# Three small VectorE steps of an attention stage put one to three steps later or earlier, and the last weight unit of the program computed in two column parts

## The chip, the cores and the metric

The kernel runs on one NeuronCore of one Trainium2 chip. The metric is the device time of one execution, in microseconds, as the median of several runs. Lower is better. Engines are named as the profile names them: PE (TensorE, matmuls) with PEld for its weight loads, DVE (VectorE), ACT (ScalarE), POOL (GpSimd), SP (SyncE, which issues the weight transfers).

## The reference, cut to what matters

A two-layer transformer on 256 tokens of width 1024, all in f32. Each layer is a SwiGLU FFN, a mixer and a second SwiGLU FFN, each followed by a layer norm of `ALPHA * x + f`. The mixer of layer 0 is the NSA attention, that of layer 1 a differential attention. The change touches the NSA attention and the very last layer norm.

```python
def post_norm(x, f, g, b):
    return layer_norm(DEEPNORM_ALPHA * x + f, g, b)      # after every FFN and mixer

# nsa_mixer, per block of queries: three branches
s = einsum('bqghd,bcgd->bqghc', qc, k_cmp)               # compressed: 15 keys per group
p_cmp = softmax(where(vis, s, NEG)) * any(vis)
o_cmp = einsum('bqghc,bcgd->bqghd', p_cmp, v_cmp)
o_slc = softmax(masked qr . k_sel) @ v_sel               # here every block is selected
o_win = softmax(masked qr . k_win) @ v_win
o = g[0] * o_cmp + g[1] * o_slc + g[2] * o_win
```

The FFN is `0.5 * (silu(x @ w_gate) * (x @ w_up)) @ w_down` with an inner width of 2816.

## The kernel before

**Tiling.** The 256 tokens are two tiles of 128 (`tok` 0 and 1). Every large matrix product is made from three fp32r matmuls: activations and weights are split in a high and a low part (`xt_hi`, `xt_lo`, `ht_hi`, `ht_lo`; `w_hi`, `w_lo`), and `three()` (L1429) issues hi·hi, hi·lo and lo·hi, 512 columns wide, into a PSUM bank of `acc`. Weights come in units of 1 MB (L438), four slots deep; ACT makes `w_hi` (L663), DVE makes `w_lo` (L961). Nine stages run one after the other: ffn0, nsa_in, nsa_out, ffn1, kv, ffn2, diff_q, diff_out, ffn3. Between nsa_in and nsa_out lies the NSA attention. Each engine has its own program, written out by hand; the engines meet at semaphores only, and each runs its instructions in order.

**The NSA attention.** `NSA_JOBS` holds 24 jobs: eight for tile 0 (two heads each), sixteen for tile 1 (one head each). `job_steps` (L114) runs 27 steps. In step i, PE computes the scores of job i (L1779, L1784, L1788), transposes the probabilities of job i-2 (`turn_p`, L1481) and multiplies those of job i-3 by the values (L1650). DVE takes the negated row maximum of job i (`maxima`, L1125), ACT takes four exponentials with their sums (`exps`, L774; they write `probs`, which lies in the tile `norm_gb`) and copies the transposed probabilities of job i-2 out of PSUM (`copy_p`, L680). Scores of job i wait for the exponentials of job i-3.

**The compressed branch of tile 1** rides along in those steps. PE computes its scores in eight pairs of heads, shared out over steps by the table `SECOND_COMPRESSED` (L1726, into bank `aux` 1). DVE adds a mask and subtracts the maximum in step 4 (`compressed_shift(1)`, L1229, L1232, L1233), ACT takes the exponential in step 4 (`compressed_exp(1)`, L867), PE transposes it in step 7, DVE copies it to `pct` (L1240). For each tile `compressed_share` (L1246 to L1248) makes the factor by which the compressed output is scaled: that of tile 0 in step 4, that of tile 1 in step 6. `split_beside(3)` cuts the rotated queries of tile 1 in high and low parts: ACT the high one in step 3 after its exponentials (L694), DVE the low one in step 3 as well (L992).

**Where a set of heads ends** (jobs 3, 7, 15, 23), DVE runs `nsa_mix` (L1257 to L1274): it inverts the sums, scales the three branches out of PSUM banks `aux` 1, `acc` 2 and `acc` 3 into SBUF, tells PE that these banks are read (`turn_read`), and adds them up. PE starts the next set with `nsa_first` (L1755), which waits for `turn_read`. The first of these mixes stands in step 6.

**POOL** meanwhile splits the four weight units of nsa_out (L567 for the high part, L568 for the low part), 16 times each.

**The end.** In ffn3, PE runs the last four units of w_down for tile 1 by halves: columns 0 to 511 of all four into `acc` 2, then columns 512 to 1023 into `acc` 3. `last_norm` (L1085) adds the residual for each half (L1094), takes `bn_stats` of it (L1097), joins the two with `bn_aggr` (L1099), and subtracts the mean while POOL makes the inverse root of the variance (L544, L547). The last line (L1108) and the output transfers (L509) follow.

Of the kernel before, what the change touches and what calls it, by code (L numbers as in the profile page):

```python
# [21 lines left out]
ALU = mybir.AluOpType  # L22
# [4 lines left out]
P = 128  # L27
# [29 lines left out]
G_FULL = FF // 512  # L57
# [41 lines left out]

SECOND_COMPRESSED = {1: range(0, 3), 2: range(3, 6), 3: range(6, 8)}  # L100

# [129 lines left out]
def build_program(nc, x_in, x_turned, const, squares_in, w_gate_up, w_downs, ln_g, ln_b, w_in, w_out_a,  # L231
                  cmp_pos, cmp_w1, cmp_b1, cmp_w2, w_kv, w_q, lambdas, subln_g, w_out_b, out):
    with ExitStack() as ctx:
# [29 lines left out]
        half_pow = sb("half_pow", [P, 4])  # L263
        stats = sb("stats", [P, 2, 6])
        mean_var = sb("mean_var", [P, TOKS, 2])
# [390 lines left out]
        def _(act):  # L656
# [213 lines left out]
            for i, sc, tr, pv in job_steps(NSA_JOBS):  # L870
# [4 lines left out]
                if sc:  # L875
                    exps("nsa", NSA_JOBS, i, 0)
                if i == 4:
                    compressed_exp(1)
# [70 lines left out]
        def _(dve):  # L949
# [135 lines left out]
            def last_norm():  # L1085
# [3 lines left out]
                for half, cols in enumerate(halves):  # L1089
                    if half == 0:  # L1090
                        dve.wait_ge(half_full, 1)
                    else:
                        filled(dve, "ffn3", G_FULL + 1, tok)
                    ins = dve.scalar_tensor_tensor(y[:, tok, cols], x[:, tok, cols], ALPHA, acc[:, 2 * tok + half],  # L1094
                                                   ALU.mult, ALU.add)
                    link(ins)
                    ins = dve.bn_stats(stats[:, half, :], y[:, tok, cols])  # L1097
                link(ins)
# [178 lines left out]
            for i, sc, tr, pv in job_steps(NSA_JOBS):  # L1277
                if sc:
                    maxima(NSA_JOBS, i, 0, score_bank[i % 3])
                if i == 0:  # L1280
                    copy_queries(1)
                if i == 4:
                    compressed_shift(1)
                if i in PCT_STEPS:
                    copy_compressed(PCT_STEPS.index(i))
                if i == 3:
                    split_beside(3)
                if i in (4, 6):
                    compressed_share(i // 2 - 2)
                if pv >= 0 and NSA_JOBS[pv][3]:  # L1290
# [137 lines left out]
        def _(pe):  # L1428
# [116 lines left out]
            def ffn_stage(stage, turn_rest, operand, next_x):  # L1545
# [35 lines left out]
                for i, js in enumerate(DOWN_GROUPS):  # L1581
# [10 lines left out]
                    if stage == "ffn3" and i == len(DOWN_GROUPS) - 1:  # L1592

                        for half in range(2):
                            for j in js:
                                ins = emit(n0 + UNITS_GU + j, j, 1, [half])
                                if half:
                                    ins.then_inc(unit_used, 1)
                            if not half:
                                ins.then_inc(half_full, 1)  # L1600
# [3 lines left out]
                    if i == len(DOWN_GROUPS) - 1:  # L1604
                        finish(1, ins)

            def nsa_out_stage():
# [427 lines left out]
```

## Time and profile before

| what | us |
|---|---|
| median of 3 runs (1036.62 to 1036.65) | 1036.63 |
| the profiled execution | 1036.8 |
| its span, from the first to the last instruction | 1034.6 |
| PE busy in it | 1016.9 |
| DVE busy / ACT busy / POOL busy | 580.0 / 480.5 / 108.0 |
| mean granted TensorE clock | 0.996 |

Times below are microseconds from the start of the span unless marked ns. A matmul's record is longer than the room it takes on PE, because matmuls are pipelined: the distance from one start to the next is what counts. The granted clock is given in parts of full speed. "idle before" and the engine and line behind "<-" say how long an engine had been idle before a row and who ended that.

### The profile page before, as it was taken

Reading aid. Unit: us, or ns where it says so; the run is one execution under the profiler, and the core shown is the slowest. Engines: PE = TensorE matmul, PEld = TensorE weight load, DVE = VectorE, ACT = ScalarE, POOL = GpSimd, SP = SyncE. Lnnn points to the kernel's source line nnn. Section 1 sums busy time; section 2 is a strip of 40 time slices with the busy share of each in tenths; the row PEclk is TensorE's granted clock in tenths of the full one; section 3 lists DMA queues with packets and bytes.
Section 4 is the critical chain, followed back from the end, with each engine's and each line's share of the span. In section 5 each row is a group of like instructions: output and inputs, shape, how many; then the busy total and the mean of one; then the engine's idle time right before and its main releaser. Section 6 shows DMA issues by size and latency. Waiting matters only on the chain.

```text
span 1034.6 us, 12671 instructions
## 1 busy us (share of the span) xinstructions
PE 1016.9 (98%) x4964; PEld 839.6 (81%) x4964; DVE 580.0 (56%) x583; ACT 480.5 (46%) x650; POOL 108.0 (10%) x141
## 2 busy tenths in 40 slices
PE   9999999999999999999999999999998999999997
PEld 7888888888788888888888888888887778888885
DVE  6655443764855654463575554462588774555443
ACT  7443432445673544452443434452467655554330
POOL 0010000223910100000012000000025110000000
PEclk9999999999999999999999999999999999999999
DMA  9676554650312655455446655455442354455431
GB/s 340 235 259 241 199 180 153 204 203 1 124 41 84 240 207 199 165 174 192 162 163 235 222 197 200 163 191 174 163 163 82 123 203 163 164 202 208 160 118 41
DMA packets 75835, 179.47 MB, mean 173 GB/s; under 512 B 3264, under 2 KB 5456, under 8 KB 75792
## 3 DMA queue, kind: packets, MB, share of 16 engines
q1 hardware_dynamic: 73312, 170.21, 47.2%
q0 software_dynamic: 2480, 8.66, 2.5%
q8 instruction: 30, 0.49, 0.2%
q14 instruction: 13, 0.11, 0.0%
HBM read 177.81 MB, written 1.05 MB: 173 GB/s over the span
## 4 chain that ended last, share of the span: by engine, by line
PE 94%; DVE 2%; ACT 2%; issue 1%; POOL 0%; POOLq 0%; DVEq 0%; ACTq 0%
PE acc L1431 27%; PE acc L1433 27%; PE acc L1432 27%; PE trb L1481 5%; PE acc L1650 2%; ACT norm_gb L774 1%; PE acc L1534 1%; PE acc L1537 1%; PE acc L1538 1%; PE aux L1694 1%; PE aux L1755 0%; PE acc L1784 0%; PE aux L1660 0%; DVE neg_max L1125 0%; ACT y L794 0%
## 5 line engine op out<-in xcount | busy, mean ns | idle before, releaser
L961 DVE TENSOR_TENSOR w_lo<-raw,w_hi 128x2048 fp32r<-128x2048 f32 x148 | 337.7, 2284 | 212.8 <-ACT w_hi L663 212.5
L663 ACT ACTIVATE w_hi<-raw 128x2048 fp32r<-128x2048 f32 x148 | 282.2, 1908 | 201.7 <-PE acc L1433 199.3
L1431 PE MATMUL acc<-w_hi,xt_hi 128*128 128x512 f32 x896 | 355.8, 397 | 1.8 <-DVE xt_lo L976 1.2
L1433 PE MATMUL acc<-w_hi,xt_lo 128*128 128x512 f32 x896 | 348.3, 389 | 0.0
L1432 PE MATMUL acc<-w_lo,xt_hi 128*128 128x512 f32 x896 | 347.5, 388 | 0.0
L1433 PEld LDWEIGHTS acc<-w_hi,xt_lo 128*128 128x128 f32 x896 | 168.2, 188 | 35.4
L1431 PEld LDWEIGHTS acc<-w_hi,xt_hi 128*128 128x128 f32 x896 | 168.4, 188 | 34.7 <-issue 2.5
L1432 PEld LDWEIGHTS acc<-w_lo,xt_hi 128*128 128x128 f32 x896 | 168.6, 188 | 31.6
L1431 PE MATMUL acc<-w_hi,ht_hi 128*128 128x512 f32 x352 | 139.6, 397 | 0.0
L1433 PE MATMUL acc<-w_hi,ht_lo 128*128 128x512 f32 x352 | 139.0, 395 | 0.0
L1432 PE MATMUL acc<-w_lo,ht_hi 128*128 128x512 f32 x352 | 139.0, 395 | 0.0
L546 POOL TENSOR_SCALAR rstd<-total 128x1 f32<-128x1 f32 x11 | 11.3, 1026 | 742.1 <-ACT aux L704 742.1
L1433 PEld LDWEIGHTS acc<-w_hi,ht_lo 128*128 128x128 f32 x352 | 66.0, 187 | 16.1
L1432 PEld LDWEIGHTS acc<-w_lo,ht_hi 128*128 128x128 f32 x352 | 66.0, 188 | 15.9
L1431 PEld LDWEIGHTS acc<-w_hi,ht_hi 128*128 128x128 f32 x352 | 66.0, 187 | 15.8
L716 ACT ACTIVATE ht_hi<-trb 128x512 f32 (+2 forms) x48 | 26.7, 557 | 107.8 <-PE trb L1481 107.8
L1037 DVE TENSOR_TENSOR ht_lo<-trb,ht_hi 128x512 f32 (+2 forms) x48 | 30.5, 642 | 71.9 <-ACT ht_hi L716 71.9
L712 ACT ACTIVATE y<-acc 128x512 f32<-128x512 f32 (+1 forms) x48 | 26.9, 563 | 69.7 <-PE acc L1433 69.7
L1032 DVE SCALAR_TENSOR_TENSOR y<-y,acc 128x512 f32<-128x512 f32 (+1 forms) x48 | 30.7, 639 | 39.4 <-ACT y L712 39.4
L704 ACT ACTIVATE aux<-y,total 128x1024 f32<-128x1024 f32 x11 | 12.3, 1120 | 54.8 <-DVE total L1013 54.8
L675 ACT ACTIVATE xt_hi<-trb 128x512 fp32r<-128x512 f32 x24 | 13.2, 596 | 41.9 <-PE trb L1481 41.9
L1481 PEld LDWEIGHTS trb<-id_r,y 128*128 128x128 f32 x200 | 24.9, 139 | 7.5 <-DVE y L992 0.6
(208 smaller groups left out, 806.5 us busy)
## 6 DMA issues: line engine op xcount, KB each, us to landing
raw<-ffn_gate_up SPq DMA_DIRECT2D x84, 1024.0 KB, 5.3
raw<-ffn_w_down SPq DMA_DIRECT2D x44, 1024.0 KB, 4.9
raw<-w_kv SPq DMA_DIRECT2D x8, 1024.0 KB, 5.0
raw<-w_in SPq DMA_DIRECT2D x6, 1024.0 KB, 5.9
raw<-ffn_gate_up SPq DMA_DIRECT2D x16, 256.0 KB, 6.1
raw<-w_out_a SPq DMA_DIRECT2D x4, 1024.0 KB, 4.8
raw<-w_q SPq DMA_DIRECT2D x4, 1024.0 KB, 5.1
raw<-w_out_b SPq DMA_DIRECT2D x4, 1024.0 KB, 5.7
```

Of the source, the lines that this page charges most:

```text
L663: act.activation(w_hi[:, slot, 0:k * c], raw[:, slot, 0:k * c], ACT.Copy).then_inc(hi_ready, 1)
L675: act.activation(dst, turned, ACT.Copy).then_inc(tr_hi, 1)
L712: act.activation(sil[:, tok, 0:c], acc[:, 2 * tok, 0:c], ACT.Silu).then_inc(silu_done, 1)
L716: act.activation(ht_hi[:, bass.ds(4 * g, k), tok * P:(tok + 1) * P], trb[:, bank, 0:k * P].rearrange("p (k c) -> p k c", c=P), ACT.Copy).t ...
L961: dve.tensor_tensor(w_lo[:, slot, 0:k * c], raw[:, slot, 0:k * c], w_hi[:, slot, 0:k * c].bitcast(F32), ALU.subtract).then_inc(lo_ready, 1)
L1032: dve.scalar_tensor_tensor(h_nat[:, tok, 0:c], sil[:, tok, 0:c], 0.5, up, ALU.mult, ALU.mult).then_inc(acc_free, 1)
L1037: dve.tensor_tensor(ht_lo[:, bass.ds(4 * g, k), tok * P:(tok + 1) * P], trb[:, bank, 0:k * P].rearrange("p (k c) -> p k c", c=P), ht_hi[:, ...
L1431: pe.matmul(out_ap, s_hi, hi, start=first, stop=False)
L1432: pe.matmul(out_ap, s_hi, lo, start=False, stop=False)
L1433: return pe.matmul(out_ap, s_lo, hi, start=False, stop=last)
L1481: ins = pe.transpose(trb[:, bank, j * P:(j + 1) * P], b, ident)
L1650: ins = pe.matmul(acc[:, 2 + m, (h % per_turn) * width:(h % per_turn + 1) * width], turned_probs[:, j % 2, k * P:(k + 1) * P], v_of(h, m, ...
```

## The change

Within the NSA steps, for DVE: `compressed_shift(1)` moves from step 4 to step 5, `split_beside(3)` from step 3 to step 4 (now behind the maximum of job 4), `compressed_share(0)` from step 4 to step 2, `compressed_share(1)` from step 6 to step 7. For ACT, `compressed_exp(1)` moves from step 4 to step 5. For PE, the second tile's compressed scores are shared over steps 2, 3 and 4 in place of 1, 2 and 3.

At the end, the last of the four units computes columns 512 to 767 first, into `acc` 3, signals, and then columns 768 to 1023 into bank `aux` 0, from zero. DVE adds the residual to all 512 columns after the first of them (columns 768 to 1023 then still lack that unit's share), takes the statistics of columns 512 to 767, then adds the `aux` part to the last 256 columns and takes their statistics. `bn_aggr` joins three groups.

```diff
-SECOND_COMPRESSED = {1: range(0, 3), 2: range(3, 6), 3: range(6, 8)}
+SECOND_COMPRESSED = {2: range(0, 3), 3: range(3, 6), 4: range(6, 8)}
...
-        stats = sb("stats", [P, 2, 6])
+        stats = sb("stats", [P, 3, 6])
... (ACT, in the NSA steps)
-                if i == 4:
+                if i == 5:
                     compressed_exp(1)
... (DVE, last_norm)
                 for half, cols in enumerate(halves):
-                    if half == 0:
-                        dve.wait_ge(half_full, 1)
-                    else:
-                        filled(dve, "ffn3", G_FULL + 1, tok)
+                    dve.wait_ge(half_full, half + 1)
                     ins = dve.scalar_tensor_tensor(y[:, tok, cols], x[:, tok, cols], ALPHA, acc[:, 2 * tok + half],
                                                    ALU.mult, ALU.add)
                     link(ins)
-                    ins = dve.bn_stats(stats[:, half, :], y[:, tok, cols])
+                    whole = cols if half == 0 else slice(512, 768)
+                    ins = dve.bn_stats(stats[:, half, :], y[:, tok, whole])
+                filled(dve, "ffn3", G_FULL + 1, tok)
+                ins = dve.tensor_tensor(y[:, tok, 768:1024], y[:, tok, 768:1024], aux[:, 0, 0:256], ALU.add)
+                link(ins)
+                ins = dve.bn_stats(stats[:, 2, :], y[:, tok, 768:1024])
                 link(ins)
... (DVE, in the NSA steps)
-                if i == 4:
-                    compressed_shift(1)
+                if i in (2, 7):
+                    compressed_share(i // 7)
                 if i in PCT_STEPS:
                     copy_compressed(PCT_STEPS.index(i))
-                if i == 3:
+                if i == 4:
                     split_beside(3)
-                if i in (4, 6):
-                    compressed_share(i // 2 - 2)
+                if i == 5:
+                    compressed_shift(1)
... (PE, the last four units of ffn3, second half)
-                                ins = emit(n0 + UNITS_GU + j, j, 1, [half])
+                                if half and j == js[-1]:
+                                    ins = last_quarters(n0 + UNITS_GU + j, j)
+                                else:
+                                    ins = emit(n0 + UNITS_GU + j, j, 1, [half])
...
+            def last_quarters(n, j):
+
+                hi, lo = weights(w_hi, n), weights(w_lo, n)
+                for quarter, bank in enumerate((acc[:, 3, 0:256], aux[:, 0, 0:256])):
+                    cols = slice(512 + quarter * 256, 768 + quarter * 256)
+                    if quarter:
+                        pe.wait_ge(stats_ready, 2 * NORM_OF["ffn3"] + 1)
+                    for k in range(2):
+                        kt = 2 * j + k
+                        ins = three(bank, ht_hi[:, kt, P:2 * P], ht_lo[:, kt, P:2 * P], hi[:, k, cols], lo[:, k, cols],
+                                    quarter == 1 and k == 0, k == 1)
+                    if quarter == 0:
+                        ins.then_inc(half_full, 1)
+                return ins
```

On DVE, NSA steps 3 to 6, before. `xt_lo` holds the low part of `split_beside(3)`, `neg_max` the maxima of jobs 4, 5 and 6, `cs` and `cmax` the compressed scores, `csum` the factors of `compressed_share`:

```order
L992 TENSOR_TENSOR xt_lo<-nq,xt_lo 128x16x64
L1125 TENSOR_REDUCE neg_max<-acc 128x4
L1229 TENSOR_TENSOR cs<-aux,cst 128x256
L1232 TENSOR_REDUCE cmax<-cs 128x16
L1233 TENSOR_TENSOR cs<-cs,cmax 128x256
L1246 TENSOR_REDUCE csum<-cs 128x16
L1247 RECIPROCAL csum<-csum 128x16
L1248 SCALAR_TENSOR_TENSOR csum<-csum,cst,gate 128x16
L1125 TENSOR_REDUCE neg_max<-aux 128x4
L1125 TENSOR_REDUCE neg_max<-acc 128x4
L1246 TENSOR_REDUCE csum<-cs 128x16
L1247 RECIPROCAL csum<-csum 128x16
```

The same place with the change, from the maximum of job 4 to the mix of the first set of heads (lines are shifted by 2):

```order
L1127 TENSOR_REDUCE neg_max<-acc 128x4
L992 TENSOR_TENSOR xt_lo<-nq,xt_lo 128x16x64
L1127 TENSOR_REDUCE neg_max<-aux 128x4
L1231 TENSOR_TENSOR cs<-aux,cst 128x256
L1234 TENSOR_REDUCE cmax<-cs 128x16
L1235 TENSOR_TENSOR cs<-cs,cmax 128x256
L1127 TENSOR_REDUCE neg_max<-acc 128x4
L1259 RECIPROCAL share<-sums 128x2x8
L1260 TENSOR_TENSOR share<-share,gate 128x2x8
L1271 TENSOR_TENSOR nq<-aux,csum 128x512
```

The three `csum` instructions of either tile are gone from this stretch: those of tile 0 now stand behind the maximum of job 2, those of tile 1 behind the maximum of job 7. The maximum of job 4 now stands ahead of the low part.

On PE, NSA steps 1 to 3, before (`aux<-kcb,y` are the compressed scores of tile 1, `trb<-id_r,norm_gb` the transposes of the probabilities):

```order
L1779 MATMUL acc<-diag_bf,id_bf 128x512
L1784 MATMUL acc<-nks,nqs 128x256 x4
L1726 MATMUL aux<-kcb,y 128x32 x3
L1779 MATMUL aux<-diag_bf,id_bf 128x512
L1784 MATMUL aux<-nks,nqs 128x256 x4
L1726 MATMUL aux<-kcb,y 128x32 x3
L1481 MATMUL trb<-id_r,norm_gb 128x128 x4
```

With the change:

```order
L1799 MATMUL acc<-diag_bf,id_bf 128x512
L1804 MATMUL acc<-nks,nqs 128x256 x4
L1799 MATMUL aux<-diag_bf,id_bf 128x512
L1804 MATMUL aux<-nks,nqs 128x256 x4
L1746 MATMUL aux<-kcb,y 128x32 x3
L1483 MATMUL trb<-id_r,norm_gb 128x128 x4
```

One group of three pairs fewer stands ahead of the first transposes of probabilities; two pairs now stand in step 4 instead.

On DVE, the last rows of the program, before:

```order
L1094 SCALAR_TENSOR_TENSOR y<-x,acc 128x512
L1097 BN_STATS stats<-y 128x6
L1094 SCALAR_TENSOR_TENSOR y<-x,acc 128x512
L1097 BN_STATS stats<-y 128x6
L1099 BN_AGGR mean_var<-stats 128x2
L1103 SCALAR_TENSOR_TENSOR y<-y,mean_var,norm_gb 128x512 x2
L1108 SCALAR_TENSOR_TENSOR x<-y,rstd,norm_gb 128x512 x2
```

With the change:

```order
L1091 SCALAR_TENSOR_TENSOR y<-x,acc 128x512
L1095 BN_STATS stats<-y 128x6
L1091 SCALAR_TENSOR_TENSOR y<-x,acc 128x512
L1095 BN_STATS stats<-y 128x6
L1097 TENSOR_TENSOR y<-y,aux 128x256
L1099 BN_STATS stats<-y 128x6
L1101 BN_AGGR mean_var<-stats 128x2
```

Two instructions of 256 columns are new, and the second BN_STATS reads 256 columns where it read 512. Only the rows from `y<-y,aux` on wait for PE's last matmul. On PE, the last six matmuls of 512 columns have become twelve of 256.

## Rows read from the trace of the kernel before

**Rows 1.** The page, part 4: the chain that ended last, by engine

```profile
PE 94%; DVE 2%; ACT 2%; issue 1%; POOL 0%; POOLq 0%; DVEq 0%; ACTq 0%
```

**Rows 2.** Timeline of PE, NSA steps: start, us, engine, line, what, [idle before]

```profile
252.54 0.83 PE L1726 MATMUL aux<-kcb,y 128*128 128x32 f32 x6 [0.51 <-DVE y L998]
...
261.48 0.82 PE L1784 MATMUL acc<-nks,nqs 128*128 128x256 f32 x4
263.65 0.66 PE L1481 MATMUL trb<-id_r,norm_gb 128*128 128x128 f32 x4 [1.35 <-ACT norm_gb L774]
264.79 0.97 PE L1481 MATMUL trb<-id_r,xt_lo 128*128 128x128 f32 x4 [0.49 <-ACT y L680]
...
270.65 1.13 PE L1755 MATMUL aux<-vcb,pct 128*128 128x512 f32 x2
...
281.23 1.12 PE L1755 MATMUL aux<-vcb,pct 128*128 128x512 f32 x2 [0.61 <-DVE y L1269]
```

**Rows 3.** Timeline of DVE, the same steps

```profile
252.31 0.68 DVE L1125 TENSOR_REDUCE neg_max<-acc 128x4 f32<-128x512 f32 x1
...
260.00 1.45 DVE L992 TENSOR_TENSOR xt_lo<-nq,xt_lo 128x1024 fp32r<-128x1024 f32 x1 [2.70 <-ACT xt_lo L694]
261.37 0.68 DVE L1125 TENSOR_REDUCE neg_max<-acc 128x4 f32<-128x512 f32 x1
...
262.87 0.84 DVE L1233 TENSOR_TENSOR cs<-cs,cmax 128x256 f32<-128x256 f32 x1
263.63 0.41 DVE L1246 TENSOR_REDUCE csum<-cs 128x16 f32<-128x256 f32 x1
...
264.91 0.69 DVE L1125 TENSOR_REDUCE neg_max<-aux 128x4 f32<-128x512 f32 x1
...
267.36 0.25 DVE L1257 RECIPROCAL share<-sums 128x16 f32<-128x16 f32 x1
267.65 1.03 DVE L1258 TENSOR_TENSOR share<-share,gate 128x16 f32<-128x16 f32 x1
...
269.32 1.28 DVE L1269 TENSOR_TENSOR y<-acc,share 128x512 f32<-128x512 f32 x2
```

**Rows 4.** Timeline of ACT, NSA steps 1 to 3

```profile
253.02 0.37 ACT L774 ACTIVATE norm_gb<-acc,neg_max 128x128 f32<-128x128 f32 x1 [0.28 <-DVE neg_max L1125]
...
255.14 0.60 ACT L680 ACTIVATE y<-trb 128x512 f32<-128x512 f32 x1 [0.61 <-PE trb L1481]
...
257.49 0.40 ACT L774 ACTIVATE norm_gb<-acc,neg_max 128x128 f32<-128x128 f32 x1
...
258.86 1.11 ACT L694 ACTIVATE xt_lo<-nq 128x1024 fp32r<-128x1024 f32 x1
```

**Rows 5.** Timeline of POOL: two of its sixteen low parts of weights

```profile
258.54 1.27 POOL L568 TENSOR_TENSOR w_lo<-raw,w_hi 128x512 fp32r<-128x512 f32 x1
...
267.38 1.27 POOL L568 TENSOR_TENSOR w_lo<-raw,w_hi 128x512 fp32r<-128x512 f32 x1
```

**Rows 6.** Busy time by stretch: us, PE, PEld, DVE, ACT, POOL, PEclk, DMA share, GB/s

```profile
265.00:266.00 1.00, 1.00 (x5) 0.89 (x4) 1.00 (x2) 0.37 (x3) 0.92 (x2) 0.50 1.02 397
```

**Rows 7.** Timeline of the end, PE and DVE

```profile
1025.47 0.39 PE L1431 MATMUL acc<-w_hi,ht_hi 128*128 128x512 f32 x1
...
1026.63 0.39 PE L1433 MATMUL acc<-w_hi,ht_lo 128*128 128x512 f32 x1
1027.06 0.69 DVE L1094 SCALAR_TENSOR_TENSOR y<-x,acc 128x512 f32<-128x512 f32 x1 [4.18 <-PE acc L1433]
...
1028.51 0.21 DVE L1099 BATCH_NORM_AGGREGATE mean_var<-stats 128x2 f32<-128x12 f32 x1
```

**Rows 8.** Timeline of PE, narrow matmuls of nsa_in; then a DVE group of 256 columns

```profile
199.14 0.30 PE L1432 MATMUL acc<-w_lo,xt_hi 128*128 128x304 f32 x1
199.28 0.30 PE L1433 MATMUL acc<-w_hi,xt_lo 128*128 128x304 f32 x1
...
L1037 DVE TENSOR_TENSOR ht_lo<-trb,ht_hi 128x256 fp32r<-128x256 f32 x8 | 3.4, 421 | 6.9 <-ACT ht_hi L716 6.9
```

## The prediction

> **What bounds the kernel now.** I read the chain of work that ended last first: it lies on PE for 94% [rows 1]. So only what lets PE start sooner, or what lies behind its last matmul, can move the time. Next I read PE's timeline for stretches in which it stood still. The NSA steps have them. PE waits 0.51 for the copies of the transposed queries ahead of the compressed scores, and after the scores of job 6 (261.48) it stands from about 262.2: 1.35 for exponentials, then 0.49 for ACT's copy [rows 2]. The reader is to look at two more things there. The clock granted to PE falls to 0.50 behind that gap [rows 6], which is 1.2 GHz of 2.4, so the rows there are long (0.97 for four transposes that take 0.66 just ahead). And the next set of heads (L1755) starts at 270.65, right when DVE has read the banks of the set before: its row at 269.32 lasts 1.28, to 270.60 [rows 2, 3]. This is the place that decides. PE is held there by DVE, so the gap and the slow clock ahead of it are already covered by a wait that DVE sets. Whoever sums up PE's idle time would count the wrong thing; DVE's timeline is to be read.
>
> DVE works without a pause from 260.00 to 270.60 [rows 3]. It sat idle 2.70 before, waiting for ACT's high part of the split queries (L694), with the maximum of job 4 standing behind that wait although its scores had long been there. By the starts of rows: low part 1.37 (to 261.37), maximum of job 4 and shift 2.26 (to 263.63), share of tile 0 1.28 (to 264.91), two maxima and the share of tile 1 2.45 (to 267.36), then the mix up to the release of the banks 3.24 (to 270.60). With the share at 1.28 both times, a maximum is (2.45 - 1.28) / 2 = 0.59 and the shift 2.26 - 0.59 = 1.67.
>
> **Part 1: DVE's steps.** Three things leave this chain: both shares, and the maximum of job 4, which now runs in DVE's idle time. From the start of the low part to the start of the mix there were 7.36 (260.00 to 267.36). Left are low part 1.37, maximum 0.59, shift 1.67, maximum 0.59, together 4.22. That is 3.14 less.
>
> The share of tile 0 goes behind the maximum of job 2. There DVE has the exponential of tile 0 ready and idles between steps, so the 1.28 delays the maximum of job 3 by some tenths only; ACT needs that maximum no sooner than 1.8 later, when it is through with jobs 1 and 2. Hidden. The share of tile 1 lands behind the maximum of job 7, between the first release and the second; see part 3.
>
> **Part 2: the start of the chain.** ACT starts the exponentials of job 1 at 253.02, set by DVE's maximum at 252.31, which stays. They take 1.37 (257.49 to 258.86, a job's exponentials without a wait). Then ACT waited 0.61 for the first transposes of probabilities [rows 4], because PE had two groups of compressed scores and a wait ahead of them. With the change PE does not meet the queries' copies before step 2, when they are done, so the 0.51 goes; and one group (0.59 by its first start to the next, within the 0.83 of its row) leaves the front. The transposes are ready at about 253.8, before ACT ends job 1 at 254.39. From there ACT has no wait: copy 0.50, job 2 1.37, copy 0.50, job 3 1.37, so the high part starts at 258.13 instead of 258.86. That is 0.73 sooner [rows 4].
>
> DVE's low part could then start at 259.27 instead of 260.00. Here POOL comes in. Its low part of a weight quarter runs from 258.54 to 259.81, and another one from 267.38 to 268.65. DVE's product of only 16 columns at 267.65 took 1.03 and ended at 268.68, with POOL's [rows 3, 5]: DVE stood until POOL was through. If the low part is held the same way, it starts at 259.81, but the 1.45 of its row is itself long (a POOL instruction was in its way then too), so part of this comes back. Bounds for the start of the chain: 0.73 sooner if nothing holds it, 0.19 if the whole 0.54 is lost and nothing comes back. I take 0.6, near the upper end, since the row's 1.45 holds a like wait already.
>
> The Trainium skill (SBUF — State Buffer, Who interferes with whom) says the pair of ports shared by VectorE and GpSimd is an exclusive lock that a VectorE instruction with two SBUF inputs needs against a GpSimd instruction that reads SBUF, and the later one fully blocks. By that rule the low part begins at 259.81 and runs unheld; the trace's 16-column row agrees. By the rule the gain of this part is about 0.5 and the whole 3.7; without a hold it would be 0.73 and the whole 4.0.
>
> **Part 3: what is late next.** With 3.14 + 0.6, the banks are released at 270.60 - 3.7 = 266.9. PE's own work up to there: scores of job 6 now at about 260.7, then two transposes, the first set's compressed output, values, scores of 7, transposes and scores of 8, which is some 5.4 by the room these take at full clock, so PE is there at about 266.1 and waits 0.8. So DVE still decides, and the gain is 3.7 and not PE's possible 4.5, which is the upper bound. The large gap goes, so I expect the clock to stay at full speed.
>
> From the first release to the second (270.65 to 281.23, with 0.61 of idle time at the end [rows 2]) the order is as before, except for the share of tile 1, 1.28 on DVE ahead of the maxima of jobs 8 and 9. ACT waits for those. It had about 1 to spare there and PE waits at the second release anyway, so some 0.3 sticks on ACT and none of it must reach PE. Bounds 0 to 0.5 lost; on the other side the second mix has a 16-column product that may meet POOL at a kinder moment, up to 0.6 gained. I take 0. Behind the attention stage PE runs the FFN units without waits, so what is gained there stays. POOL's splitting and the loads behind it do not depend on the moved steps.
>
> **Part 4: the end.** Before: six matmuls, 1025.47 to 1026.63 by starts, 0.232 apart; DVE's residual add at 1027.06, `bn_aggr` at 1028.51, 1.45 later [rows 7]. Matmuls of 304 columns stand 0.14 apart [rows 8]. From 0.14 and 0.232 by columns, 256 would be 0.12. So twelve take 1.44, as long as six of 512 (1.39). The first part's sixth starts at 1025.47 + 0.60 = 1026.07 and is out 0.29 later; DVE's add of 512 runs 1026.40 to 1027.11, statistics of 256 then take about 0.35 of room, DVE is free at 1027.46. The last matmul is out at 1025.47 + 1.32 + 0.29 = 1027.08, so it is DVE that is late. Then the add of 256 (0.42 for this width [rows 8], with the link 0.45) and statistics 0.44: `bn_aggr` at 1028.35, 0.16 sooner. Bounds: at 0.14 a matmul the add starts at 1027.6 and the gain is 0.0; if statistics of 256 take half of 512 (0.35), it is 0.3. With 0.04 for a third group in `bn_aggr`, I take 0.1. PE's new wait for the statistics of tile 0 is long met (that sum is done some 7 before), so nothing queues behind it.
>
> **Sum.** 3.14 + 0.6 + 0 + 0.1 = 3.8. The profiled execution took 1036.8 and would take 1033.0; the median is 1036.63, so 1032.8.
>
> **Rivals.**
>
> (a) Given back behind the first release. The share of tile 1 makes ACT late for jobs 8 and 9, the second mix is late by as much, and POOL holds two more DVE instructions for up to 1.0 each. Price 0.5 + 1.0 and more: a gain of 1.0 to 2.2, time 1034.4 to 1035.6. For it: ACT's slack there is under the 1.28. Against it: the 0.61 of idle time on PE and ACT's pauses in later steps. 13%.
>
> (b) The clock falls again. PE still waits about 0.8 at 266.1. If the grant goes to 0.50 there for some 3.3 (as before, when it was back at full clock by 269), 1.65 is lost and this time nothing covers it: gain 2.2, time 1034.5. For it: the fall stood behind gaps of 1.35 and 0.49. Against it: behind 0.61 alone, L1755 takes 1.12 at 281.23, as long as at 270.65 where the clock was back [rows 2]. 6%.
>
> (c) Slower than before. The same fall, but lasting: every microsecond at 1.2 GHz in the attention steps costs up to 0.5, so from 7.6 of it on the 3.8 are spent, and at 12 the time is 1036.63 - 3.8 + 6 = 1038.8. The trace shows no fall that long. 2%, and 1% for any other slowdown.
>
> (d) More than expected: the low part is not held and the two 16-column products meet no POOL instruction (0.8 each). The chain then ends sooner than PE, PE's own work decides, 4.5 + 0.6 at the second release + 0.2 at the end: 5.3, time 1031.3. 10%.
>
> (e) The moves do not do what they say, because PE and not DVE holds 270.65 (the slow clock). Then only 1.84 of gap and the slow clock's share go and the time depends on them: by 1.84 + 1.7 it is 1033.1, which the total can't tell from my case; the row at the first release can. 8%.
>
> **Chances.** Forecast 60%, 1032.8 with its own range 1032.0 to 1033.9; (a) 13, (b) 6, (c) 3, (d) 10, (e) 8. A measurement of this kernel can tell about 0.2%, 2.07, from no change, so 1034.56 is the line: faster takes the forecast, (d), (e), and about half of (a) and (b), 87%; same 10%; slower 3%. The range reaches to 1031.6 and 1034.5.
>
> **What would show it.** DVE's chain: the maximum of job 4 ahead of the low part; the low part at 259.3 to 259.8; the release at 266.9 and L1755's counterpart right behind. ACT without a wait between jobs 1 and 3. Full clock throughout. The second release 10.6 after the first. At the end `bn_aggr` 0.1 to 0.2 sooner against the twelve matmuls' first start. I am wrong if PE arrives at the first release with no wait, if the second release comes over 11 after the first, or if the matmuls of 256 columns stand 0.15 or more apart.

## The result, and where the time went

The changed kernel takes 1027.43 us (median of 4 runs, 1027.19 to 1027.63) where the kernel before takes 1036.62 (4 runs, 1036.44 to 1036.65): ratio 0.9912, interval 0.9900 to 0.9924. That is 9.2 us less. Forecast was 1032.8 with a range of 1031.6 to 1034.5, so the time lies outside the range, by 4.2, on the good side. The profiled execution took 1027.5 with a span of 1025.6, against a span of 1034.6 before.

I cut both spans at three points of PE's timeline that exist in both traces: the first compressed score of tile 1 (L1726, now L1746), the first matmul of nsa_out, and the first matmul of the last six (now twelve).

| stretch | before | after | difference |
|---|---|---|---|
| start to first compressed score (ffn0, nsa_in) | 245.56 | 244.01 | -1.55 |
| from there to nsa_out's first matmul (attention) | 65.81 | 63.24 | -2.57 |
| from there to the last unit's second half | 714.10 | 709.32 | -4.78 |
| from there to the last `bn_aggr` | 3.04 | 2.88 | -0.16 |
| from there to the end of the span | 6.09 | 6.15 | +0.06 |
| span | 1034.6 | 1025.6 | -9.0 |

Two cuts of the kernel before, from PE's timeline (start, us, engine, line, what), that the rows ahead of the prediction don't hold:

```profile
245.56 1.86 PE L1726 MATMUL aux<-kcb,y 128*128 128x32 f32 x16
...
311.37 0.48 PE L1431 MATMUL acc<-w_hi,xt_hi 128*128 128x512 f32 x1
```

And PE's timeline of the changed kernel (in brackets the idle time before a row, and who ended it):

```profile
244.01 1.86 PE L1746 MATMUL aux<-kcb,y 128*128 128x32 f32 x16
...
265.42 1.13 PE L1775 MATMUL aux<-vcb,pct 128*128 128x512 f32 x2 [0.81 <-DVE y L1271]
...
270.57 0.63 PE L1483 MATMUL trb<-id_r,norm_gb 128*128 128x128 f32 x4 [1.26 <-DVE pct L1242]
...
276.60 1.12 PE L1775 MATMUL aux<-vcb,pct 128*128 128x512 f32 x2
...
280.66 0.66 PE L1483 MATMUL trb<-id_r,norm_gb 128*128 128x128 f32 x4 [0.17 <-ACT norm_gb L774]
...
307.25 0.48 PE L1433 MATMUL acc<-w_hi,xt_hi 128*128 128x512 f32 x1
```

The table says at once that the prediction missed something: 1.55 is gone ahead of the first instruction that the change moves, and 4.78 in stages whose instructions it leaves alone. Both stretches hold FFNs, one in the first and three in the third, and 1.6 for each fits both.

**What is faster there.** PE's groups by form (line, engine, what, count; busy us, mean ns of one; idle before), before:

```profile
L1431 PE MATMUL acc<-w_hi,xt_hi 128*128 128x512 f32 x880 | 350.9, 399 | 1.8 <-DVE xt_lo L976 1.2 <-ACT norm_gb L774 0.6
...
L1433 PE MATMUL acc<-w_hi,xt_lo 128*128 128x512 f32 x880 | 343.5, 390 | 0.0
...
L1431 PE MATMUL acc<-w_hi,ht_hi 128*128 128x512 f32 x352 | 139.6, 397 | 0.0
L1433 PE MATMUL acc<-w_hi,ht_lo 128*128 128x512 f32 x352 | 139.0, 395 | 0.0
L1432 PE MATMUL acc<-w_lo,ht_hi 128*128 128x512 f32 x352 | 139.0, 395 | 0.0
```

The same view of the changed kernel:

```profile
L1433 PE MATMUL acc<-w_hi,ht_hi 128*128 128x512 f32 x350 | 136.9, 391 | 0.0
L1434 PE MATMUL acc<-w_lo,ht_hi 128*128 128x512 f32 x350 | 136.2, 389 | 0.0
L1435 PE MATMUL acc<-w_hi,ht_lo 128*128 128x512 f32 x350 | 136.2, 389 | 0.0
```

Matmuls whose weight load reads `ht_hi` or `ht_lo` (w_down's, in all four FFNs) have become 6 ns shorter on all three lines: 397, 395 and 395 before, 391, 389 and 389 after. Those on `xt_hi` and `xt_lo` have the same means in both kernels (399, 389 and 390; the 399 is the line that also holds the waits). Starts say the same. Before, PE's timeline near the end has the `ht` matmuls 0.234 apart (8 steps from the first to the last of these rows, 1.87):

```profile
1009.37 0.40 PE L1431 MATMUL acc<-w_hi,ht_hi 128*128 128x512 f32 x1
...
1011.24 0.40 PE L1433 MATMUL acc<-w_hi,ht_lo 128*128 128x512 f32 x1
```

After, they are 0.226 apart (5 steps from 1015.21 to 1016.34, first two rows below). There are 1056 of them, and 1056 x 6 ns is 6.3, which is 1.55 + 4.78.

The instructions are the same. What differs is where their operands lie. `stats` grew from 48 to 72 bytes per partition, and everything allocated behind it moved by 32 bytes, `ht_hi` from 179040 to 179072 and `ht_lo` from 201568 to 201600 among it (addresses in the built programs). So they began 32 bytes past a multiple of 64 and now begin at one. `w_hi` (49280), `w_lo` (82048), `xt_hi` (131200) and `xt_lo` (139392) lie ahead of `stats`, at multiples of 64 in both kernels.

**The end**, timelines of PE and DVE, changed kernel:

```profile
1015.21 0.39 PE L1433 MATMUL acc<-w_hi,ht_hi 128*128 128x512 f32 x1
...
1016.34 0.39 PE L1435 MATMUL acc<-w_hi,ht_lo 128*128 128x512 f32 x1
1016.57 0.28 PE L1433 MATMUL acc<-w_hi,ht_hi 128*128 128x256 f32 x1
1016.68 0.28 PE L1434 MATMUL acc<-w_lo,ht_hi 128*128 128x256 f32 x1
...
1017.49 0.69 DVE L1091 SCALAR_TENSOR_TENSOR y<-x,acc 128x512 f32<-128x512 f32 x1 [3.33 <-PE acc L1435]
...
1017.88 0.28 PE L1435 MATMUL aux<-w_hi,ht_lo 128*128 128x256 f32 x1
1018.21 0.43 DVE L1095 BATCH_NORM_STATS2 stats<-y 128x6 f32<-128x256 f32 x1
1018.55 0.40 DVE L1097 TENSOR_TENSOR y<-y,aux 128x256 f32<-128x256 f32 x1
1018.99 0.43 DVE L1099 BATCH_NORM_STATS2 stats<-y 128x6 f32<-128x256 f32 x1
1019.45 0.24 DVE L1101 BATCH_NORM_AGGREGATE mean_var<-stats 128x2 f32<-128x18 f32 x1
```

Twelve starts from 1016.57 to 1017.88 are 0.12 apart, DVE is the late one, and `bn_aggr` stands 2.88 behind the first of them, where it stood 3.04 behind [rows 7]. It takes 0.24 for three groups, 0.03 more than for two.

**The attention.** DVE's timeline, changed kernel, from the low part on:

```profile
257.75 1.64 DVE L992 TENSOR_TENSOR xt_lo<-nq,xt_lo 128x1024 fp32r<-128x1024 f32 x1 [1.23 <-ACT xt_lo L694]
...
262.29 1.16 DVE L1260 TENSOR_TENSOR share<-share,gate 128x16 f32<-128x16 f32 x1
...
264.09 1.28 DVE L1271 TENSOR_TENSOR y<-acc,share 128x512 f32<-128x512 f32 x2
265.40 1.03 DVE L1275 TENSOR_TENSOR nq<-nq,y 128x512 f32<-128x512 f32 x1
266.46 1.65 DVE L1276 TENSOR_TENSOR nq<-nq,y 128x512 f32<-128x512 f32 x1
268.03 0.68 DVE L1127 TENSOR_REDUCE neg_max<-acc 128x4 f32<-128x512 f32 x1
268.63 0.40 DVE L1248 TENSOR_REDUCE csum<-cs 128x16 f32<-128x256 f32 x1
...
270.00 0.42 DVE L1242 COPY pct<-trb 128x256 f32<-128x256 f32 x1
```

Measured from the first compressed score, so that the faster FFN ahead drops out, the first release comes at 21.41 (265.42 - 244.01) where it came at 25.09 [rows 2]: 3.68 sooner. The second comes at 32.59 where it came at 35.67: 3.08 sooner. nsa_out begins 2.57 sooner. So 0.6 is given back before the second release and 0.5 behind it. The rows show two candidates: DVE has no pause from 265.40 to 270.4. Its two adds take 1.03 and 1.65, the share of tile 1 (L1248 and two more) comes next, 1.37 long by the starts of rows, and PE waits 1.26 for the copy to `pct` behind it. In the kernel before, where POOL was splitting weights as well, the same two adds were 1.01 shorter in all, and no share stood behind them:

```profile
270.63 0.69 DVE L1273 TENSOR_TENSOR nq<-nq,y 128x512 f32<-128x512 f32 x1
271.36 0.98 DVE L1274 TENSOR_TENSOR nq<-nq,y 128x512 f32<-128x512 f32 x1
```

The granted clock held. Window over the attention stretch, changed kernel (us; busy PE, PEld, DVE, ACT, POOL with counts; clock; DMA share; GB/s):

```profile
245.00:311.00 66.00, 63.23 (x477) 54.68 (x477) 44.57 (x73) 45.91 (x165) 35.49 (x38) 1.00 0.25 80
```

### The profile page after: what moved, and what is told of

The parts are those of the page before. It is cut to its first block, busy times and chain, and to the rows that moved or that the text cites. A ratio compares the mean times of both kernels' runs of the same rounds, so it can differ in the third digit from the quotient of the medians.

```text
span 1025.6 us, 12685 instructions
## 1 busy us (share of the span) xinstructions
PE 1008.6 (98%) x4970; PEld 838.6 (82%) x4970; DVE 581.7 (57%) x585; ACT 479.8 (47%) x650; POOL 108.1 (11%) x141
## 4 chain that ended last, share of the span: by engine, by line
PE 93%; DVE 3%; ACT 2%; issue 1%; DMA 1%; POOL 0%; SPq 0%; POOLq 0%; DVEq 0%; ACTq 0%
PE acc L1433 28%; PE acc L1435 27%; PE acc L1434 27%; PE trb L1483 5%; PE acc L1670 1%; ACT norm_gb L774 1%; PE acc L1536 1%; PE acc L1539 1%; PE acc L1540 1%; PE aux L1714 1%; DMA raw<-ffn_gate_up 1%; DVE neg_max L1127 0%; PE acc L1804 0%; DVE y L1271 0%; ACT y L794 0%
## 5 line engine op out<-in xcount | busy, mean ns | idle before, releaser
L1433 PE MATMUL acc<-w_hi,ht_hi 128*128 128x512 f32 x352 | 137.4, 390 | 0.0
L1434 PE MATMUL acc<-w_lo,ht_hi 128*128 128x512 f32 x352 | 136.8, 389 | 0.0
L1435 PE MATMUL acc<-w_hi,ht_lo 128*128 128x512 f32 x352 | 136.8, 389 | 0.0
```

Of the source, the lines that this page charges most:

```text
L1433: pe.matmul(out_ap, s_hi, hi, start=first, stop=False)
L1434: pe.matmul(out_ap, s_hi, lo, start=False, stop=False)
L1435: return pe.matmul(out_ap, s_lo, hi, start=False, stop=last)
```

## Experiments

Each was run in turn with the kernel before on the same chip. The medians of that one were 1036.76 in the first batch, 1036.53 in the second and 1036.61 in the third.

### First batch: is it the places, and whose

`e1` gives the kernel before the wider `stats` and nothing else. `e2` is the changed kernel with two small buffers allocated as one, so that all behind them lies where it lay before. `e3` puts 32 unused bytes ahead of `ht_hi` in the kernel before; `e4` puts them ahead of `xt_hi`, and 32 more behind `xt_lo`, so that only the two `xt` buffers (and what lies behind by a whole 64) move.

```diff
 e1_wide_stats (against before)
-        stats = sb("stats", [P, 2, 6])
+        stats = sb("stats", [P, 3, 6])
...
-        dve.bn_aggr(mean_var[:, tok, :], stats[:].rearrange("p a b -> p (a b)"))
+        dve.bn_aggr(mean_var[:, tok, :], stats[:, 0:2].rearrange("p a b -> p (a b)"))
 e2_after_old_places (against after)
-        mean_var = sb("mean_var", [P, TOKS, 2])
...
-        rstd = sb("rstd", [P, TOKS, 2])
+        pair = sb("pair", [P, TOKS, 4])
+        mean_var, rstd = pair[:, :, 0:2], pair[:, :, 2:4]
 e3_pad_ht (against before)
+                sb("pad", [P, 8], scope=ffn)
                 ht_hi = sb("ht_hi", [P, FT, SEQ], F32R, ffn)
 e4_pad_xt (against before)
+        sb("pad_a", [P, 8])
         xt_hi = sb("xt_hi", [P, KT, SEQ], F32R)
         xt_lo = sb("xt_lo", [P, KT, SEQ], F32R)
+        sb("pad_b", [P, 8])
```

> The kernel before with one line of the change: the tile `stats` gets room for three groups in place of two (72 bytes a partition for 48; only two are used). Everything that is allocated behind it, `ht_hi` and `ht_lo` among it, then starts 32 bytes further on, at multiples of 64 bytes. Theory L (layout): the 1056 matmuls whose stationary operand is `ht_hi` or `ht_lo` stand 0.227 apart in place of 0.233, in all four FFNs; 1036.6 - 6.3 = 1030.3. Rival S (the moved steps and the end made all of the 9.2): 1036.6, no change.

Measured: 1030.23 (1030.17 to 1030.60), ratio 0.9936 [0.9919, 0.9952]. One number in the size of a buffer of 48 bytes is worth 6.5 us.

> The changed kernel whole, but `mean_var` and `rstd` share one tile of 32 bytes, so that all buffers behind them lie where they lay before. Theory L: only the moved steps (2.6 by the trace) and the end (0.16) are left, 1036.6 - 2.8 = 1033.8, and the matmuls on `ht` stand 0.233 apart. Rival S: 1027.4 as with the change.

Measured: 1033.87 (1033.48 to 1034.02), ratio 0.9970 [0.9959, 0.9982]. All moved steps and the new end without the new places bring 2.9. Together with e1 that is 9.4, against 9.2 for the whole change: the two parts add up. From the first compressed score, the first release comes at 21.37 (266.75 - 245.38) and nsa_out at 63.16, as in the changed kernel.

> The kernel before with 32 unused bytes ahead of `ht_hi`, so that only `ht_hi` and `ht_lo` move to multiples of 64; the attention's buffers stay. Theory L (it is the stationary operand of the down projection): as e1, 1030.3. Rival T (another buffer behind `stats` matters, those of the attentions): 1036.6, or part of the way.

Measured: 1030.05 (1029.85 to 1030.45), ratio 0.9935 [0.9918, 0.9952]. The same gain without touching `stats`: it is the `ht` buffers, not `stats` or one of the small ones behind it.

> The kernel before with 32 bytes ahead of `xt_hi` and 32 behind `xt_lo`: `xt_hi` and `xt_lo` start 32 bytes past a multiple of 64, the buffers behind move by 64. If theory L holds for any stationary operand, the 2784 matmuls on `xt` (0.227 apart) go to 0.233: +17, 1053.5. If the place matters for `ht` alone for another reason (its size, its strides, its neighbours): 1036.6.

Measured: 1051.35 (1051.27 to 1051.48), ratio 1.0140 [1.0123, 1.0157]. The cost can be moved to the `xt` matmuls, and there, with 2736 of 512 columns, it is 14.6 us, or 5.3 ns for each. PE's groups by form, e4:

```profile
L1433 PE MATMUL acc<-w_hi,xt_hi 128*128 128x512 f32 x880 | 355.4, 404 | 1.8 <-DVE xt_lo L978 1.2 <-ACT norm_gb L776 0.6
...
L1435 PE MATMUL acc<-w_hi,xt_lo 128*128 128x512 f32 x880 | 348.0, 395 | 0.0
```

399 and 390 have become 404 and 395.

### Second batch: which rule, and the parts of the change alone

So far a rule "the buffer of the weight load must start at a multiple of 64" fits (the theories with an L in the expectations are of that kind). `e5` moves `w_hi` and `w_lo`, which PE reads as the moving operand, to 32 past such a multiple and leaves all others. `e6` moves `ht_hi` alone to a multiple of 64. `e8` has the moved steps alone, `e9` the new end alone, both with the places of before.

```diff
 e5_pad_w (against before)
+        sb("pad_a", [P, 8])
         w_hi = sb("w_hi", [P, SLOTS, UNIT], F32R)
         w_lo = sb("w_lo", [P, SLOTS, UNIT], F32R)
+        sb("pad_b", [P, 8])
 e6_ht_hi_only (against before)
+                sb("pad_a", [P, 8], scope=ffn)
                 ht_hi = sb("ht_hi", [P, FT, SEQ], F32R, ffn)
+                sb("pad_b", [P, 8], scope=ffn)
                 ht_lo = sb("ht_lo", [P, FT, SEQ], F32R, ffn)
 e8_steps_only (against after): last_norm, the last unit and stats as before
-        stats = sb("stats", [P, 3, 6])
+        stats = sb("stats", [P, 2, 6])
...
-                                if half and j == js[-1]:
-                                    ins = last_quarters(n0 + UNITS_GU + j, j)
-                                else:
-                                    ins = emit(n0 + UNITS_GU + j, j, 1, [half])
+                                ins = emit(n0 + UNITS_GU + j, j, 1, [half])
 e9_end_only (against before): those three as in the changed kernel, and pair of e2
```

> The kernel before with 32 bytes ahead of `w_hi` and 32 behind `w_lo`: the moving operand of nearly all matmuls (`w_hi`, `w_lo`) starts 32 bytes past a multiple of 64, all stationary operands stay where they were. Theory L1 (only where the stationary operand starts matters): 1036.7. Theory L2 (each operand that PE reads matters alike): 3840 matmuls at 0.006 more, 1060.

Measured: 1044.75 (1044.71 to 1045.17), ratio 1.0078 [1.0061, 1.0095]. PE's groups by form, e5:

```profile
L1433 PE MATMUL acc<-w_hi,xt_hi 128*128 128x512 f32 x880 | 355.4, 404 | 1.8 <-DVE xt_lo L978 1.2 <-ACT norm_gb L776 0.6
...
L1433 PE MATMUL acc<-w_hi,ht_hi 128*128 128x512 f32 x352 | 137.6, 391 | 0.0
```

This was in neither expectation. The `xt` matmuls, at a multiple of 64, have become slow, and the `ht` ones, still 32 past one, fast. In numbers: +14.6 as in e4 and -6.5 as in e3 make +8.1, and +8.2 was measured. No rule on one operand gives that. A rule on both does: the matmul is fast when the buffer of its weight load and that of its moving operand begin alike, both at a multiple of 64 or both 32 past one. I called this M and let the third batch try it.

> The kernel before with 32 bytes ahead of `ht_hi` and 32 between it and `ht_lo`: `ht_hi` starts at a multiple of 64, `ht_lo` does not. Of three matmuls two load `ht_hi` and one `ht_lo`. If each load of a badly placed operand costs its own 6 ns: two thirds of the 6.5 of e1 and e3 are gained, 1036.7 - 4.4 = 1032.3. If one bad load in a group of three spoils all: 1036.7. If only the first load of a group counts: 1030.1.

Measured: 1036.34 (1036.07 to 1036.99), ratio 0.9998 [0.9989, 1.0008]. No gain at all, although two of three weight loads now read a buffer that begins like `w_hi` and `w_lo`. PE's groups by form, e6:

```profile
L1434 PE MATMUL acc<-w_lo,ht_hi 128*128 128x512 f32 x352 | 140.7, 400 | 0.0
L1433 PE MATMUL acc<-w_hi,ht_hi 128*128 128x512 f32 x352 | 139.6, 396 | 0.0
L1435 PE MATMUL acc<-w_hi,ht_lo 128*128 128x512 f32 x352 | 137.0, 389 | 0.0
```

The means have shifted between the three lines and their sum hardly (1185 ns; 1187 before, 1169 after). By starts too the cost is not spread evenly: from `w_hi,ht_hi`, `w_lo,ht_hi` and `w_hi,ht_lo` to the next start the trace has 232, 239 and 228 ns on average (steps over 300 ns left out), where the kernel before has 233 each.

> The moved steps of the NSA attention alone, on the kernel before; the end and all places as before. By the trace of the changed kernel: 1036.7 - 2.6 = 1034.1. If steps and end together (e2, 1033.9) are more than the steps alone by more than 0.5, the end is worth more than its 0.16.

Measured: 1033.95 (1033.63 to 1034.45), ratio 0.9974 [0.9964, 0.9984]. From the first compressed score: first release 21.40, nsa_out 63.19. The moved steps alone are the whole of the 2.6.

> The end alone (last unit in two column parts, third group of statistics), all places and steps as before. By the rows at the end of the changed kernel `bn_aggr` is 0.16 sooner after the start of the last unit: 1036.5. Rival: the narrow matmuls or the third group cost something that the one profile hides, 1036.7 or more.

Measured: 1036.41 (1036.10 to 1036.99), ratio 0.9998 [0.9988, 1.0007]. The trace has `bn_aggr` 2.87 behind the first of the twelve, so the 0.16 is there; the times don't resolve it.

This trace shows one thing more. Its attention steps are those of the kernel before, with the same two gaps on PE (1.34 and 0.49), but the granted clock stays at 1.00 behind them, where it fell to 0.50 before. PE's timeline, e9:

```profile
265.33 1.02 PE L1775 MATMUL aux<-vcb,pct 128*128 128x512 f32 x2
...
270.75 1.12 PE L1775 MATMUL aux<-vcb,pct 128*128 128x512 f32 x2 [1.41 <-DVE y L1271]
```

PE is early by 1.41 and waits, and the first release comes 25.12 behind the first compressed score (270.75 - 245.63), as the 25.09 of the kernel before. So the slow clock there cost nothing, as the prediction said: DVE set that time. Of the profiles with the old steps, e1, e4, e6 and e12 have the fall (1.75 to 1.92 for the first set's pair of compressed outputs) and e3, e5, e9 and e13 do not (1.02); their releases all lie 25.07 to 25.12 behind the first compressed score.

### Third batch: both operands, and what was given back

`e12` puts `w`, `xt` and `ht` all 32 past a multiple of 64: by M as good as e1, by any rule that wants a multiple of 64 the worst of all. `e13` is e6 turned round, `ht_lo` alone like `w`. `e10` and `e11` start from the changed kernel and ask who gave time back behind the first release: the share of tile 1 in DVE's chain (G in the expectations; e10 puts it from step 7 to step 11), or POOL's splits, which stand in the way of DVE's adds (P; e11 besides lets POOL begin them only behind the first mix).

```diff
 e12_all_at_32 (against before)
+        sb("pad_a", [P, 8])
         w_hi = sb("w_hi", [P, SLOTS, UNIT], F32R)
...
+                sb("pad_b", [P, 8], scope=ffn)
                 ht_hi = sb("ht_hi", [P, FT, SEQ], F32R, ffn)
 e13_ht_lo_only (against before)
                 ht_hi = sb("ht_hi", [P, FT, SEQ], F32R, ffn)
+                sb("pad_b", [P, 8], scope=ffn)
                 ht_lo = sb("ht_lo", [P, FT, SEQ], F32R, ffn)
 e10_late_share (against after)
-                if i in (2, 7):
-                    compressed_share(i // 7)
+                if i in (2, 11):
+                    compressed_share(i // 11)
 e11_pool_late (against after): e10, and
+            pool.wait_ge(turn_mixed, 1)
             split_units(UNIT_OF["nsa_out"], UNIT_OF["nsa_out"] + 4)
```

> The kernel before with `w_hi`, `w_lo`, `xt_hi`, `xt_lo`, `ht_hi` and `ht_lo` all 32 bytes past a multiple of 64. Theory M (what matters is that the stationary and the moving operand start alike modulo 64, as e5 suggests, where `ht` and `w` both at 32 stood 0.227 apart): all matmuls 0.227 apart, 1030.2 as e1 and e3. Theory L (each stationary operand has to start at a multiple of 64): at least e4's 1051. Theory L2 (both operands cost their own): above that.

Measured: 1030.04 (1029.94 to 1030.36), ratio 0.9936 [0.9919, 0.9953], as e1 and e3. PE's groups by form, e12:

```profile
L1433 PE MATMUL acc<-w_hi,xt_hi 128*128 128x512 f32 x880 | 350.9, 399 | 1.8 <-DVE xt_lo L978 1.2 <-ACT norm_gb L776 0.6
...
L1433 PE MATMUL acc<-w_hi,ht_hi 128*128 128x512 f32 x352 | 137.6, 391 | 0.0
```

M holds: none of the six buffers begins at a multiple of 64 and all matmuls are fast. Whether 64 is the right period is not settled. In every run the buffers of a fast pair lie a multiple of 128 bytes apart, and those of a slow pair 32 more or 32 less than one. No run has them 64 apart, so a rule of 128 bytes fits as well as M with its 64.

> The kernel before with 32 bytes between `ht_hi` and `ht_lo`: now only `ht_lo`, a third of the loads, starts like the weights. With e6, where two thirds did and nothing was gained. If any load that differs spoils its group of three: 1036.5. If the number of like loads counted: 1034.4.

Measured: 1036.86 (1036.37 to 1037.47), ratio 1.0000 [0.9991, 1.0010]. Like e6: a group of three in which one or two loads are unlike costs what a group of three unlike ones costs, here again unevenly (236, 233 and 231 ns to the next start). Why, I can't say.

> The changed kernel with `compressed_share(1)` on DVE in step 11 in place of step 7, behind the second release. In the changed kernel it stands, 1.28 long, in a DVE chain without a pause from the first release to the copy of `pct` for which PE waits 1.26. Theory G (this share gives back part of the gain): PE waits for the copy no more, 0.6 to 1.0 off, 1026.4 to 1026.8. Rival (the second release waits for PE's scores anyway): 1027.4.

Measured: 1027.32 (1026.80 to 1027.50), ratio 0.9909 [0.9893, 0.9926]; the changed kernel has 1027.43. PE's timeline, e10:

```profile
269.62 0.66 PE L1483 MATMUL trb<-id_r,norm_gb 128*128 128x128 f32 x4 [0.99 <-ACT norm_gb L774]
...
279.75 0.66 PE L1483 MATMUL trb<-id_r,norm_gb 128*128 128x128 f32 x4 [0.41 <-ACT norm_gb L774]
...
286.32 0.63 PE L1483 MATMUL trb<-id_r,nq 128*128 128x128 f32 x4 [0.24 <-DVE xt_lo L976]
```

The wait of 1.26 for `pct` is gone, and one of 0.99 for ACT stands in its place: ACT's exponentials of job 7 wait for a maximum that DVE takes behind the two adds. With the share in step 11, PE waits 0.41 and 0.24 there, where it waited 0.17. The second release comes 10.80 behind the first (275.54 - 264.74), 0.38 sooner than the 11.18 of the changed kernel, but the waits behind it take that back. In all PE waits 2.43 from the first release on (0.79, 0.99, 0.41, 0.24), against 2.24 in the changed kernel (0.81, 1.26, 0.17), and the attention stretch is 63.47, not shorter than 63.24. Moving the share from step 7 to step 11 gains nothing. That doesn't clear it: it stands in DVE's chain in both places, and no run leaves it out.

> As e10, and POOL starts to split the weights of nsa_out only when the first mix is done. Theory P (DVE's instructions with two inputs in SBUF stand while POOL works): the low part of the queries takes 1.2 in place of 1.64, the product of 16 columns 0.2 in place of 1.16, the two adds of the first mix 0.7 each in place of 1.03 and 1.65; the first release is then set by PE, 0.8 sooner, and another 1 goes behind it; the third mix now meets POOL and loses up to 1. Net 0.5 to 1.5 under e10. Rival (those durations are DVE's own): as e10, and rows unchanged.

Measured: 1025.73 (1025.37 to 1026.16), ratio 0.9895 [0.9878, 0.9912]: 1.6 below e10 and 1.7 below the changed kernel, with no overlap of the runs. DVE's timeline, e11:

```profile
257.45 1.23 DVE L993 TENSOR_TENSOR xt_lo<-nq,xt_lo 128x1024 fp32r<-128x1024 f32 x1 [1.23 <-ACT xt_lo L695]
...
261.32 0.17 DVE L1261 TENSOR_TENSOR share<-share,gate 128x16 f32<-128x16 f32 x1
...
263.76 0.69 DVE L1276 TENSOR_TENSOR nq<-nq,y 128x512 f32<-128x512 f32 x1
264.48 0.69 DVE L1277 TENSOR_TENSOR nq<-nq,y 128x512 f32<-128x512 f32 x1
...
274.38 1.64 DVE L1277 TENSOR_TENSOR nq<-nq,y 128x512 f32<-128x512 f32 x1
```

With POOL quiet, the instructions that read two operands from SBUF take 1.23, 0.17, 0.69 and 0.69; in the changed kernel, with POOL at work, the same four take 1.64, 1.16, 1.03 and 1.65. At 274.38 POOL is back, and the same add takes 1.64 again. Instructions of DVE that read PSUM or a single operand don't change: a maximum takes 0.68 and the scaling of a PSUM bank (L1272) 0.69 in both. PE waits at neither release; behind them only 0.23, 0.23 and 0.17 are left, and the stretch is 61.57 long. The second release comes 9.44 behind the first. POOL's splitting now ends at 298.5 and is still ahead of nsa_out, at 305.28. This version is faster than both kernels.

## Why the prediction was wrong, point by point

**The step that failed** is in the sum (3.14 + 0.6 + 0 + 0.1), by absence. It put nothing on the stages whose instructions stay; of them it said only that what is gained stays there. But the change makes `stats` larger, and the prediction priced only the instructions of the third group. That a buffer's size moves all buffers behind it was not asked, so the largest term is missing: the `ht` matmuls of the four FFNs give 6.3 of the 9.0 by which the span is shorter, and e1, with the wider buffer alone, gives 6.5. A hint was in the same trace: part 4 took 0.232 between matmuls from [rows 7], while `xt` matmuls of the same shape and line stand 0.227 apart (243.97 to 245.33 in six steps). Two distances for one form of instruction is a question, and I used one as a constant.

**Part 1 and the DVE chain: right.** First release 3.68 sooner for 3.7 predicted, and the steps alone (e8) put it at the same place. PE comes to it with 0.81 of waiting, for 0.8 predicted, so it is DVE that holds it, and rival (e), that PE does, is out (e9 says the same of the old steps). The 3.7 itself is met partly by luck, because small misses cancel. The low part's start is 0.1 better than taken, and its room on DVE is 1.56 where 1.37 was taken. The subtraction of the compressed maxima (L1235) takes 0.68 where it took 0.84, and the 16-column product 1.16 where it took 1.03. All three are shorter still with POOL quiet (1.23, 0.42 and 0.17 in e11).

**Part 2: right.** ACT has no wait between jobs 1 and 3. DVE's low part starts at 13.74 from the first compressed score (257.75 - 244.01), where it stood at 14.44 (260.00 - 245.56): 0.70 sooner for 0.6 taken. The prediction reckoned with a start held back until POOL's low part ends. But its row begins while that one runs, from 257.02 to 258.30, and lasts 1.64, where it takes 1.23 with POOL quiet (e11): the hold shows as a longer row, not as a later start. POOL's timeline, changed kernel:

```profile
257.02 1.28 POOL L568 TENSOR_TENSOR w_lo<-raw,w_hi 128x512 fp32r<-128x512 f32 x1
258.26 1.61 POOL L567 CAST w_hi<-raw 128x512 fp32r<-128x512 f32 x1
```

POOL's next instruction is in turn the long one, 1.61 where others of its kind take 0.61. That both sides are held in turn is what the Trainium skill (SBUF — State Buffer, Who interferes with whom) calls an exclusive lock. e11 shows what it is worth here to keep POOL quiet up to the end of the first mix: 1.9 of the attention stretch and 1.6 of the time, against e10. How long an instruction is held depends on where POOL's own stand: with POOL at work too, the first add took 0.69 in the kernel before, and the product of the second mix 0.17 in e10.

**Part 3: size wrong.** I took 0 for what is given back behind the first release, with 0.5 as the worst; it is 1.1. Rival (a) named both mechanisms that the rows show, POOL holding DVE's instructions and the share of tile 1 on DVE ahead of the next maxima. The adds are 1.01 longer than before and the share is 1.37 of room that was not there. How the 1.1 divides between them is open: e11 shows that the holding is worth more than that 1.1, but takes away holds that the kernel before had too, and e10 moves the share and does not remove it. Without the new places, steps and end take 1033.87 (e2) and the steps alone 1033.95 (e8), where 1032.8 was forecast: a gain of 2.9 and 2.6 against the kernel before, for 3.8. The second release comes 11.18 behind the first, for 10.6 predicted, and over the 11 that I had named as the sign of being wrong. That sign did its work.

**The clock: right.** 1.00 through the stretch. Rivals (b) and (c) are out; a wait of 1.26 and one of 0.81 brought no fall. The reason given, that the large gap goes, is weaker than it looked: e3, e5, e9 and e13 have the old gaps and no fall either.

**Part 4: right.** 256 columns are 0.12 apart, `bn_aggr` 0.16 sooner as worked out. With 0.03 of it given back in `bn_aggr` itself, 0.1 to the end of the span, as taken.

By terms: 3.7 + 0 + 0.1 was forecast, and 3.7 - 1.1 + 0.1 = 2.7 came of it; 6.3 came from places.

## What to carry to other kernels

When a change resizes, adds or drops a buffer, however small, look at where all buffers behind it now begin, and price that apart from the instructions; one run of the old kernel with the new size alone (e1) tells it. Compare the distance between like matmuls over different operands: where one form has two distances, something other than its shape sets it, and here 32 bytes of padding (6.5) were worth over twice the moved steps (2.6). Ahead of moving steps of an engine along a chain, see whether the long ones among them are long by themselves: keeping POOL away from the two-input DVE instructions, of 0.17 to 0.69, that took 1.03 to 1.65 beside it was worth 1.6, and moving the share once more nothing.

## What was not expected of the hardware

- An fp32r matmul of 512 columns takes 0.227 of PE's time when the buffers of its loaded and its moving operand begin alike modulo 64 bytes, and 0.232 to 0.234 when one begins 32 bytes off. Both at 0: e1, e3 (1030.2, 1030.1). Both at 32: e12 (1030.0). Unlike for `ht`: 1036.6. Unlike for `xt`: e4 (1051.35) has `w` at 0 and `ht` unlike as well, and e5 (1044.75) has `w` and `ht` at 32. Offsets other than 32, a distance of 64, and other types weren't tried, and what in the chip makes the difference is not known.
- In groups of three matmuls, one unlike load (e6) or two (e13) cost as much as three. Why stays open.
- A DVE product of 16 columns takes 0.17 alone and up to 1.16 beside POOL; an add of 512 columns 0.69 and up to 1.65 (e11 against the changed kernel).
- The start of the program scatters: kernels in which all FFN matmuls are fast reach the first compressed score between 243.35 and 244.18, and those in which only the `ht` ones are slow between 245.38 and 246.01. What a change does behind that is read from that point, not from the start; e10's 0.1 against the changed kernel is such a scatter.
- With the old steps, the same two gaps on PE (1.34 or 1.35, then 0.48 or 0.49) were followed by a fall of the granted clock to 0.50 in the profile of the kernel before and by none in those of e3, e5, e9 and e13. A fall seen in one profile need not be in the next.
